# Up projection of a float32 hybrid layer: pairs 7 and 14 join one run of twenty seven-product pairs

## The reference, cut to what matters

```python
h2 = _rmsnorm(x, g_ffn)
f = jnp.einsum("btd,df->btf", h2, w_up)              # 1024 -> 2 * 2816
f_gate, f_up = jnp.split(f, [D_FF], axis=-1)
f_conv, new_f = _causal_dwconv(f_gate, buf_f, conv_f_w)   # 3 taps along the tokens
x = x + jnp.einsum("btf,fd->btd", jax.nn.silu(f_conv) * f_up, w_down)
y = _rmsnorm(x, g_final)
```

## Time and profile before

| | |
|---|---|
| median of 3 runs | 840.9 us (840.87 to 841.06) |
| the profiled execution's own time | 840.82 us |
| span of the profile, first to last instruction | 839.0 us |
| TensorE matmul busy | 829.2 us, 99% |
| weight loads busy | 825.3 us, 98% |
| VectorE busy | 715.0 us, 85% |
| ScalarE busy | 431.6 us, 51% |
| GpSimd busy | 145.2 us, 17% |
| mean granted TensorE clock | 0.998 |

### The profile page before, as it was taken

How to read it: one execution, slowest core, us unless ns; L and a number is a source line. 1 busy time by engine, 2 the same in 40 slices (tenths; PEclk the granted TensorE clock), 3 DMA queues, 4 the chain that set the end, 5 groups by cost and what they waited for, 6 DMA issues and landing times.

```text
span 839.0 us, 18038 instructions
## 1 busy us (share of the span) xinstructions
PE 829.2 (99%) x6853; PEld 825.3 (98%) x6853; DVE 715.0 (85%) x1076; ACT 431.6 (51%) x782; POOL 145.2 (17%) x114
## 2 busy tenths in 40 slices
PE   8999999999999999999999999999999999999996
PEld 7999999999999999999999999999999999999996
DVE  4899898989999976666569899989999998977775
ACT  7753636454333234764236566556655666633443
POOL 2283847566000000000003200000000002500000
PEclk9999999999999999999999999999999999999999
DMA  9423323432342342326933124333342334334553
GB/s 263 127 77 111 91 81 94 134 117 88 100 118 80 100 112 76 95 82 76 202 107 92 50 60 118 101 102 101 103 125 78 109 95 129 102 94 103 120 111 106
DMA packets 188158, 88.73 MB, mean 106 GB/s; under 512 B 34168, under 2 KB 186636, under 8 KB 188068
## 3 DMA queue, kind: packets, MB, share of 16 engines
q1 hardware_dynamic: 183921, 86.02, 38.2%
q10 hardware_dynamic: 4171, 1.82, 0.8%
HBM read 83.79 MB, written 3.51 MB: 104 GB/s over the span
## 4 chain that ended last, share of the span: by engine, by line
PE 97%; DVE 1%; ACT 1%; issue 0%; ACTq 0%; DVEq 0%
PE psum L2123 36%; PE psum L2129 18%; PE psum L2293 17%; PE psum L2298 9%; PE psum L2426 6%; PE psum L2321 4%; PE psum L2432 3%; PE psum L2326 2%; PE psum L2498 1%; PE psum L2166 1%; PE psum L2173 0%; PE psum L2164 0%; PE psum L2101 0%; PE psum L2515 0%; PE psum L2238 0%
## 5 line engine op out<-in xcount | busy, mean ns | idle before, releaser
L2123 PE MATMUL psum<-act,w_hi 128*128 128x260 f32 x1984 | 258.5, 283 | 0.0
L2123 PEld LDWEIGHTS psum<-act,w_hi 128*128 128x128 f32 x1984 | 246.3, 188 | 0.0
L2129 PE MATMUL psum<-act,w_lo 128*128 128x260 f32 x992 | 139.9, 283 | 0.0
L1305 DVE TENSOR_TENSOR w_lo<-raw,w_hi 128x1024 fp32r<-128x1024 f32 x78 | 102.0, 1309 | 35.3 <-ACT w_hi L704 35.0
L2129 PEld LDWEIGHTS psum<-act,w_lo 128*128 128x128 f32 x992 | 128.0, 188 | 0.0
L644 POOL TENSOR_TENSOR gate_a<-gate_a,prods 128x512 f32<-128x512 f32 x72 | 109.5, 1521 | 80.9 <-ACT prods L789 72.6
L2293 PE MATMUL psum<-act,w_hi 128*128 128x260 f32 x704 | 111.4, 282 | 0.7 <-ACT tmp L1056 0.7
L2293 PEld LDWEIGHTS psum<-act,w_hi 128*128 128x128 f32 x704 | 96.7, 188 | 0.9 <-ACT tmp L1056 0.9
L1604 DVE TENSOR_TENSOR w_lo<-raw,w_hi 128x1024 fp32r<-128x1024 f32 (+1 forms) x68 | 81.6, 1203 | 16.2 <-ACT w_hi L977 16.1
L704 ACT ACTIVATE w_hi<-raw 128x1024 fp32r<-128x1024 f32 x78 | 82.0, 1053 | 21.4 <-PE psum L2129 16.7
L977 ACT ACTIVATE w_hi<-raw 128x1024 fp32r<-128x1024 f32 (+1 forms) x68 | 69.6, 1030 | 40.9 <-PE psum L2298 25.9
(11 more groups left out here) (270 smaller groups left out, 1247.0 us busy)
## 6 DMA issues: line engine op xcount, KB each, us to landing
raw<-in_w_in SPq DMA_DIRECT2D x56, 512.0 KB, 3.8
raw<-in_w_up SPq DMA_DIRECT2D x44, 512.0 KB, 3.8
raw<-in_w_down SPq DMA_DIRECT2D x16, 448.0 KB, 3.8
v<-in_x_prompt SPq DMA_DIRECT2D x8, 512.0 KB, 7.5
raw<-in_w_b_out SPq DMA_DIRECT2D x8, 512.0 KB, 4.0
raw<-in_w_a_out SPq DMA_DIRECT2D x8, 512.0 KB, 6.0
raw<-in_w_o SPq DMA_DIRECT2D x8, 512.0 KB, 4.4
raw<-in_w_down SPq DMA_DIRECT2D x8, 512.0 KB, 4.1
```

The lines of the kernel that those rows point to most:

```text
L1305: ve.tensor_tensor(w_lo[:, slot, 0:k, :], raw[:, s, 0:k, :], w_hi[:, slot, 0:k, :], ALU.subtract).then_inc(lo_done, 1)
L2123: pe.matmul(a[:, h, :], w_hi[:, s, j, :], rhs(k, part)[:, h * H:(h + 1) * H], start=start and part == 0, stop=False)
L2129: last = pe.matmul(a[:, h, :], w_lo[:, s, j, :], rhs(k, 0)[:, h * H:(h + 1) * H], start=False, stop=stop)
```

## The change

`PLAIN` loses pairs 7 and 14, so pairs 1 to 20 are one run of seven-product pairs: step 6 becomes `step_in_run`, so do 7, 8, 13, 14 and 15; only step 20 ends a run. The bank tables are redone for it. The five early splits are spread over steps 6, 8, 10, 12 and 14, one each, on ScalarE and VectorE. The root row moves from the end of plain step 7 to the end of seven-product step 7, and `turn_root` from the end of step 14 to the end of step 13. Every low part is made on VectorE, as before. SyncE's loads and GpSimd's work keep their order.

```diff
--- before.py
+++ after.py
@@ -69,14 +69,15 @@
 
     KH = KT // 2
     SUMS_IN = ("B11", "B12", "T1", "B21", "B22", "T2", "T3", "T4")
-    PLAIN = (0, 7, 14, 21)
+    PLAIN = (0, 21)
 
     DOWN = [(kind == "s", int(j)) for kind, j in ("p0", "p1", "p2", "p3", "s0", "p4", "s1", "p5", "s2", "p6", "s3", "p7")]
     JOBS = FT + len(DOWN)
     SEVEN = [n not in PLAIN for n in range(FT)] + [seven for seven, _ in DOWN]
     JOB_P = [FT + DOWN.index((False, j)) for j in range(KT)]
     JOB_S = [FT + DOWN.index((True, m)) for m in range(KT // 2)]
-    EARLY = {7: (0, 1, 2), 14: (3, 4)}
+    EARLY = {6: (0,), 8: (1,), 10: (2,), 12: (3,), 14: (4,)}
+    ROOT_ROW, ROOT_TURN = (7, 13)
     EARLY_HI = sum(len(t) for t in EARLY.values())
     Z_AT = ((3 * KT, 3 * KT + 1), (3 * KT + 2, 2 * FT - 1))
 
@@ -388,9 +389,8 @@
         assert not any(FOLLOWS[FT:]) and not SEVEN[-1]
         assert PLAIN[0] == 0 and PLAIN[-1] == FT - 1 and SEVEN[1]
 
-        BANK_X = {1: 2, 2: 3, 3: 0, 4: 1, 5: 0, 6: 3, 8: 2, 9: 0, 10: 3, 11: 0, 12: 3, 13: 0, 15: 0, 16: 3, 17: 1, 18:
-                  3, 19: 1, 20: 3}
-        BANK_GATE = {0: 0, 7: 0, 14: 1, 21: 0}
+        BANK_X = {1: 2, 2: 3, 3: 0, 4: 1, 5: 2, 6: 3, 7: 0, 8: 1, 9: 2, 10: 3, 11: 0, 12: 1, 13: 2, 14: 3, 15: 0, 16: 1, 17: 2, 18: 3, 19: 2, 20: 3}
+        BANK_GATE = {0: 0, 21: 0}
         assert len(BANK_X) + len(BANK_GATE) == FT
 
         def bank_x(n):
@@ -1141,6 +1141,8 @@
                 silu(n - 1)
                 up_5(n)
                 hi_2(n + 1)
+                for i in EARLY.get(n, ()):
+                    up_hi(i)
 
             def step_at_end_of_run(n):
 
@@ -1798,11 +1800,6 @@
                 weight_sum_4(n + 1)
                 for i in EARLY.get(n, ()):
                     up_lo(i)
-                if n == PLAIN[1]:
-                    ve.transpose(halves(x_root_row)[:, :, 0:HB], spread(roots)).then_inc(norm_turned, 1)
-                    ve.tensor_scalar(halves(x_root_row)[:, :, HB:H], few(roots), 1.0, None, ALU.mult).then_inc(norm_set, 1)
-                if n == PLAIN[2]:
-                    turn_root()
 
             def step_of_second(n):
 
@@ -1848,6 +1845,13 @@
                 weight_sum_3(n + 1)
                 up_22(n)
                 weight_sum_4(n + 1)
+                for i in EARLY.get(n, ()):
+                    up_lo(i)
+                if n == ROOT_ROW:
+                    ve.transpose(halves(x_root_row)[:, :, 0:HB], spread(roots)).then_inc(norm_turned, 1)
+                    ve.tensor_scalar(halves(x_root_row)[:, :, HB:H], few(roots), 1.0, None, ALU.mult).then_inc(norm_set, 1)
+                if n == ROOT_TURN:
+                    turn_root()
 
             def step_at_end_of_run(n):
```

## The result

The changed kernel takes **845.82 us** (median of four runs, 845.74 to 845.92) against 840.88 us before on the same chips (840.76 to 841.06, four runs). The ratio is 1.0058, with a 95% interval of 1.0046 to 1.0070: 4.9 us slower. The forecast was 845.1 us, in a range of 843.2 to 847.4. The profiled execution took 845.92 us, with a span of 843.8 us.

What follows compares the result with a forecast made beforehand. VectorE was taken to bound the long run: 17 steps of 10.23 us plus 5.76 us of insertions put TensorE's P4 of pair 19 4.32 us later, so 840.82 + 4.32 = 845.1 us, range 843.2 to 847.4.

Steps and rivals of the forecast that it cites:

- The bound: In seven-product steps VectorE sets the pace, 10.23 us a step; TensorE's own pace is 10.12, losing 0.11 us a pair.
- TensorE's part: Pairs 2 to 19: 24 fewer matmuls save 2.9 us; at TensorE's own pace P4 of pair 19 comes 3.31 us earlier.
- VectorE's part: Steps 3 to 19: 17 x 10.23 = 173.91 us plus 5.76 for five splits, root row and turn_root; 4.32 us later.
- The waits: TensorE waits for lo_2 in P6, where 0.35 us of an insertion goes unnoticed, and for lo_3 in P7, without room.
- What I cost at nothing: Early high parts on ScalarE, new banks and SyncE's loads add nothing; without cover each high part would cost some 0.6 us.
- The end of the run: From P4 of pair 19 to pair 21: adds nothing, 8.67 us now against 8.66 at the end of the first run.
- TensorE sets the pace throughout: Rival: TensorE bounds the whole run, so the gain of 3.31 us arrives, 837.5 us; chance 0.04.
- Insertions hidden in VectorE's waits: Rival: operations inserted in the run cost nothing, only VectorE's pace counts, 1.44 us less, 839.4 us; chance 0.04.
- The clock: Rival: clock falls while turn_root leaves TensorE idle in pair 14, 2.9 us more, 848 us; chance 0.02.
- Resynchronising: Rival: after each of seven insertions it costs more than one wait of 0.33 us, time above 847.4 us; chance 0.03.
- The low end of the range: VectorE's 10.23 us step may hold 0.11 us of waiting that an insertion fills: 1.9 us less, 843.2 us.

Runs made afterwards that it cites:

- best2: Changed kernel with up_gate's operations and the taps parted, turn_root in the down projection, root row and one early split behind the run, four splits respaced: 837.86 us.
- turn_late: Changed kernel with turn_root alone moved out of step 13 into the down projection: 843.31 us, ratio 1.0029 to the kernel before.
- interleave: Changed kernel with the same VectorE operations reordered, the two of up_gate and the two convolution taps parted by others: 841.49 us, ratio 1.0008 to the kernel before.
- after_extra17: Changed kernel with one more 128x520 VectorE addition at the end of step 17: 846.44 us, ratio 1.0068 to the kernel before.
- before_extra10: Kernel before with one more 128x520 VectorE addition at the end of step 10, in its second run: 840.76 us, ratio 0.9999.
- turn_mid: Changed kernel with turn_root inside step 13, in front of weight_sum_3 instead of at the step's end before up_gate: 845.43 us, ratio 1.0054 to the kernel before.

## Why the prediction was right

**The bound.** VectorE's pace, 10.23 us a step, held in the whole run, and TensorE followed it at 0.09 to 0.10 us' distance up to pair 19. That was read from three steps of the first run in the profile before; the rest of that profile (two runs at 10.12 us) pointed the other way, and best2 shows that this other way was real as well, with VectorE's load cut.

**TensorE's part.** The 24 matmuls went and their 2.9 us were not seen in the changed kernel. They are seen in best2, where P4 of pair 19 stands at 684.90; the forecast put TensorE's own pace at 685.04.

**VectorE's part.** Predicted 17 x 10.23 + 5.76 = 179.67 us from step 3 to step 20; measured 693.12 - 513.08 = 180.04. The splits at 0.61 to 0.62 and the root row at 0.67 us were right to the hundredth. The term that was too small is `turn_root`: 2.04 predicted, 2.47 measured. Its price was taken where a different operation stood behind it. The run as a whole came out 0.37 us longer than predicted, about half of the 0.7 us by which the forecast of the median was low. Another 0.3 us lies outside the span. The forecast took for granted that this part stays as it is; every run on record shows that it does not, and the cause stays open.

**The waits.** P6 and P7 wait, as was said, for `lo_2` and `lo_3`. Behind `turn_root` a third place appeared that I had not named: P6 waits for the snapshot of P1's bank, which ScalarE may write only when VectorE's `cx` sum has read the last one. It costs nothing beyond the rest, since VectorE is late by the same amount at each of these places.

**What I cost at nothing.** The early high parts on ScalarE, the new banks and the loads: no wait of VectorE on any of them shows in the run, and best2, which has the new banks and the early high parts too, keeps 10.12 us a pair. The end of the run cost nothing either, 8.67 us from P4 of pair 19 to pair 21 as before.

**The rivals.** That TensorE sets the pace throughout is refuted by turn_late, interleave and after_extra17. By the rule of the Trainium skill that was weighed there (Perfetto Trace Analysis, Identifying the Most-Contended Engine) the busiest engine by weight loads is TensorE, with 98% in both profiles; measured, moving 2.5 us of work out of the run on the engine with 86% took 2.5 us off the time. The same page of the Trainium skill (section Optimization Strategy) says that the most contended engine can change from one regime of a kernel to the next. Taken stretch by stretch the rule agrees with the changed kernel, where from 503 to 693 us VectorE is busy 188.13 us and the weight loads 183.50. It does not agree with the first run of the kernel before, where VectorE set the pace with 48.48 us busy against 48.87 for the weight loads: when two engines are this close, the order of their busy times does not name the one that sets the pace. Insertions hidden in VectorE's waits: refuted, each is paid. The clock did not fall; the granted clock is 1.00 from 628 to 645 us, around `turn_root`. Resynchronising: the seven insertions cost 0.4 us more than their sum, not 2.3.

One choice needs a remark. The low end of the range rested on the 0.11 us by which VectorE's step exceeds TensorE's being waiting that an insertion could fill. The interleaved step shows that there was time to win, 0.26 us a step (10.23 less 9.97). But it lies between an operation and the one that needs its result, and an insertion between steps does not fill it; only an operation between those two does.

## What to carry to other kernels

Two engines within about 1% of each other: compare their periods in one repeating step, not their busy shares, and follow the lead of the one over the other from step to step. A run that is cheap while short can be the bound when long, because what stood between the runs was refilling the lead; before removing it, add up the work of the other engine over the whole new run, insertions included. Then look whether that engine can be made faster by order alone: parting dependent pairs of operations turned 4.9 us lost into 0.7, and putting `turn_root`, the root row and one of the splits where there is room turned it into 2.9 gained.

## What the runs showed of the hardware

A VectorE operation of 520 columns that reads the result of the one right before it starts 0.72 to 0.73 us after that one (690.67 to 691.40), while independent ones of that size follow at 0.61. With the two dependent pairs of a step parted, the step went from 10.23 to 9.97 us. The Trainium skill (VectorE: DVE Perf Modes, The DRAIN you can't avoid) reports that a chain of eight copies takes the same time with a semaphore behind each as with one behind the last. The trace agrees: the independent operations here raise a semaphore too and follow at 0.61 us, and the added operation of before_extra10, which raises none, is followed after the same 0.61 (594.74 to 595.35). What costs 0.11 to 0.12 us is that the next operation waits for the result of the one right before it. Whether the wait or the dependence itself costs it was not separated.

Behind `turn_root`, whose last five operations take 0.09 to 0.21 us each, VectorE stood idle for 0.38 us before an operation that waits for four semaphores, and not at all before one that waits for none (turn_mid) or for one (interleave). In the kernel before, `plain_gate` with three waits followed it without such a gap, so the count of waits alone does not settle it; this stays open.
